# First FFN's pairs 5 to 17 as seven block products, and modulation pieces moved between stages

## The reference, cut to what matters

```python
mod = cond @ w_ada[l] + b_ada[l]
sh1, sc1, gt1, sh2, sc2, gt2, sh3, sc3, gt3 = ...   # nine rows of 1024
u = modulate(rms_norm(h, g_ffn1[l]), sh1, sc1)
h = h + 0.5 * gt1 * swiglu(u, w_ffn1_in[l], w_ffn1_out[l])
u = modulate(rms_norm(h, g_mix[l]), sh2, sc2)
h = h + gt2 * hybrid_mixer(u, w_in[l], ...)         # attention and gated delta net
u = modulate(rms_norm(h, g_ffn2[l]), sh3, sc3)
h = h + 0.5 * gt3 * swiglu(u, w_ffn2_in[l], w_ffn2_out[l])

def swiglu(u, w_in, w_out):
    a, b = jnp.split(u @ w_in, 2, axis=-1)          # 1024 -> 2 x 2816
    return (jax.nn.silu(a) * b) @ w_out
```

## Time and profile before

| | |
|---|---|
| median of 3 runs | 1198.42 us (1197.99 to 1198.63) |
| the profiled execution's own time | 1196.75 us |
| its span, first to last instruction | 1195.0 us |
| TensorE busy | 1179.7 us of 1195.0 |
| granted TensorE clock | 0.999 over the span |
| DVE, ACT busy | 826.4 us, 556.9 us |

### The profile page before, as it was taken

The page is one execution under the profiler, slowest core; times in us unless marked ns, Lnnn a source line. Parts: engine busy times, 40 slices in busy tenths (PEclk is TensorE's granted clock), DMA queues, the critical chain, the costliest instruction groups (busy, mean ns, idle before and its releaser), DMA issues.

```text
span 1195.0 us, 20070 instructions
## 1 busy us (share of the span) xinstructions
PE 1179.7 (99%) x7503; PEld 993.5 (83%) x7503; DVE 826.4 (69%) x1219; ACT 556.9 (47%) x843; POOL 60.3 (5%) x98
## 2 busy tenths in 40 slices
PE   7999999999999999999999999999999999999998
PEld 5788888888888887777787878888889999998887
DVE  5666676665665694777587566666789999988552
ACT  5423232322222585676773536544446666653331
POOL 1000000000111000000402110003000000000000
PEclk9999999999999999999999999999999999999999
DMA  9777666776564233221233132653233333342440
GB/s 326 230 205 210 199 176 187 210 211 192 160 167 115 56 104 89 71 54 53 71 89 91 53 96 66 211 153 95 71 106 106 106 105 103 102 132 78 115 115 27
DMA packets 235053, 152.51 MB, mean 128 GB/s; under 512 B 8021, under 2 KB 216046, under 8 KB 234990
## 3 DMA queue, kind: packets, MB, share of 16 engines
q1 hardware_dynamic: 230890, 149.62, 43.4%
q10 hardware_dynamic: 4100, 2.02, 0.6%
HBM read 145.31 MB, written 6.29 MB: 127 GB/s over the span
## 4 chain that ended last, share of the span: by engine, by line
PE 93%; DVE 3%; ACT 2%; DMA 1%; issue 1%; SPq 0%; ACTq 0%; DVEq 0%
PE tail L2224 8%; PE tail L2228 7%; PE tail L2233 7%; PE region L2224 7%; PE region L2233 7%; PE region L2228 7%; PE tail L2214 5%; PE region L2315 5%; PE region L2319 5%; PE region L2312 5%; PE tail L2216 5%; PE tail L2215 5%; PE region L2214 2%; PE region L2216 2%; PE region L2215 2%; PE tail L2312 1%
## 5 line engine op out<-in xcount | busy, mean ns | idle before, releaser
L785 ACT ACTIVATE w_hi<-raw 128x1024 fp32r<-128x1024 f32 (+1 forms) x160 | 179.1, 1119 | 359.7 <-PE region L2233 161.3
L1366 DVE TENSOR_TENSOR w_lo<-raw,w_hi 128x1024 fp32r<-128x1024 f32 (+1 forms) x158 | 205.9, 1303 | 92.5 <-ACT w_hi L785 92.4
L2214 PE MATMUL tail<-u_hi,w_hi 128*128 128x512 f32 x264 | 107.6, 408 | 0.9 <-DVE w_lo L1366 0.9
L2216 PE MATMUL tail<-u_hi,w_lo 128*128 128x512 f32 x264 | 103.2, 391 | 0.0
L2215 PE MATMUL tail<-u_lo,w_hi 128*128 128x512 f32 x264 | 103.0, 390 | 0.0
L2224 PE MATMUL region<-u_hi,w_hi 128*128 128x512 f32 x368 | 91.1, 390 | 0.1
L2233 PE MATMUL region<-u_hi,w_lo 128*128 128x512 f32 x368 | 90.9, 389 | 0.0
L2228 PE MATMUL region<-u_lo,w_hi 128*128 128x512 f32 x368 | 90.9, 389 | 0.0
L2224 PEld LDWEIGHTS region<-u_hi,w_hi 128*128 128x128 f32 x368 | 68.9, 188 | 15.2 <-issue 0.6
L2228 PEld LDWEIGHTS region<-u_lo,w_hi 128*128 128x128 f32 x368 | 69.1, 188 | 14.4
L2233 PEld LDWEIGHTS region<-u_hi,w_lo 128*128 128x128 f32 x368 | 69.1, 188 | 14.3
(11 more groups left out here) (492 smaller groups left out, 2332.7 us busy)
## 6 DMA issues: line engine op xcount, KB each, us to landing
raw<-in_w_ffn_in SPq DMA_DIRECT2D x168, 256.0 KB, 3.5
ada_raw<-in_w_ada SPq DMA_DIRECT2D x56, 512.0 KB, 5.2
raw<-in_w_in SPq DMA_DIRECT2D x90, 256.0 KB, 3.3
raw<-in_w_ffn_out SPq DMA_DIRECT2D x32, 384.0 KB, 5.3
raw<-in_w_ffn_out SPq DMA_DIRECT2D x32, 320.0 KB, 4.5
ada_early<-in_w_ada SPq DMA_DIRECT2D x8, 1024.0 KB, 10.7
gates<-kept_gates SPq DMA_DIRECT2D x16, 256.0 KB, 2.9
raw<-in_w_out SPq DMA_DIRECT2D x16, 256.0 KB, 3.2
```

Source lines behind the costliest of these rows:

```text
L785: act.activation(w_hi[:, slot % 2, 0:k, :], raw[:, slot, 0:k, :], ACT.Copy).then_inc(hi_ready, 1)
L1366: dve.tensor_tensor(w_lo[:, slot % 2, 0:k, :], raw[:, slot, 0:k, :], w_hi[:, slot % 2, 0:k, :].bitcast(f32), ALU.subtract).then_inc(lo_rea ...
L2214: pe.matmul(bank(b), wh, xh, start=start and n == 0, stop=False)
L2216: ins = pe.matmul(bank(b), wl, xh, start=False, stop=stop and n == k - 1)
```

## The change

Pairs 5 to 17 of the first FFN are mixed as those of the second. Their token sums are made at its start: `full` is written by ACT with the same activation that makes `u_hi` (8 activations in the chunk loop), the four sums, their splits and the copies stand in pairs 1 to 3. The modulation pieces leave pairs 1, 5 to 16; they stand one, two and one in pairs 2, 3, 4, then 2, 3, 4, 4, 3 in pairs 17 to 21, four in each of seven outputs, two around the merge and six in W_OUT. `ada_raw` has four buffers, its totals are added in four batches, and the rounds change their order. The loops of the first FFN keep only pairs 6 to 15 rolled.

```diff
-MOD_ROUNDS = (0, FF // P // 2 - 1, (MODS * KD - LATE) // 4)
+ROUNDS = (MODS * KD - LATE) // 4
+ROUND_AT = (0, 1, 4, 5, 2, 3) + tuple(range(6, ROUNDS))
+MOD_ROUNDS = (0, 4, 6, ROUNDS - 2, ROUNDS)
+PIECES = {2: (0,), 3: (1, 2), 4: (3,), 17: (4, 5), 18: (6, 7, 8), 19: (9, 10, 11, 12), 20: (13, 14, 15, 16), 21: (17, 18, 19)}
+OUT_PIECE = 20
+LAST_PIECE = OUT_PIECE + 4 * (D // P - 1)
...
-MIX_0, MIX_LAST = 5, KF - 1
+FULL_STEPS = KD, KD // 2
+MIX_0, MIX_LAST = (5, 5), (17, KF - 1)
...
-    return f == 1 and (not is_static(i) or MIX_0 <= 2 * i + jj <= MIX_LAST)
+    return not is_static(i) or MIX_0[f] <= 2 * i + jj <= MIX_LAST[f]
...
-                ada_raw = sb("ada_raw", [P, 2, ROWS, 4 * P], stack=t)
+                ada_raw = sb("ada_raw", [P, 4, ROWS, 4 * P], stack=t)
...
+                    for q in PIECES.get(2 * i + u // 2, ())[2 * (u % 2):2 * (u % 2) + 2] if is_static(i) else ():
+                        if q == 0:
+                            sp.wait_ge(t_step, tokens_done(0, FULL_STEPS[0] + 4))
+                        if q == 6:
+                            sp.wait_ge(glu_ready, MIX_LAST[0] + 1)
+                        load_piece(q, piece_slot(q), q % 4)
...
-                        load_late(2 * KF + 4 * i + u - 2, u % 2, (u - 2) % 4)
+                        for k in range(2):
+                            slot = (2 * u + k) % 4
+                            load_piece(OUT_PIECE + 8 * i + 2 * u + k, slot, slot)
...
+                if n == W_OUT:
+                    sp.wait_ge(unit_done, W_OUT)
+                if n in (MERGE, MERGE + 1) or W_OUT <= n < W_OUT + 6:
+                    q = LAST_PIECE + (n - MERGE if n < W_OUT else 2 + n - W_OUT)
+                    load_piece(q, piece_slot(q), q % 4)
...
                     early_part(k + 2)
+                for k1 in (k, k + 1):
+                    act.activation(full[0][:, k1, :], work[:, k1 % 2, :], ACT.Identity,
+                                   bias=mod[:, SH[0] * KD + k1:SH[0] * KD + k1 + 1]).then_inc(t_step, 1)
+                if k + 2 < KD:
...
+            def tokens(f, j, place):
+
+                if not is_static(j):
+                    return
+                for n in ((0,), (1,), (2, 3))[place]:
+                    if j == 1 + f:
+                        token_sums(f, n)
+                    if f and j == 3:
+                        tokens_lo(f, n)
+                if f == 0 and j in (2, 3) and place:
+                    tokens_lo(f, 2 * (j - 2) + place - 1)
...
+            def in_pieces(j):
+
+                for q in PIECES.get(j, ()):
+                    if q and q % 4 == 0:
+                        ada_rows(q // 4 - 1)
+                    piece(q, piece_slot(q), q % 4)
+
+            def out_pieces(o, slots):
+
+                for slot in slots:
+                    piece(OUT_PIECE + 4 * o + slot, slot, slot)
+
+            def last_piece(n):
+
+                q = LAST_PIECE + n
+                piece(q, piece_slot(q), q % 4)
+                if q % 4 == 3:
+                    ada_rows(q // 4)
...
+            ada_rows(OUT_PIECE // 4 - 1)
...
+            last_piece(0)
...
+            last_piece(1)
...
+                    if o < 6:
+                        last_piece(2 + o)
...
+                if k:
+                    dve.wait_ge(t_step, k - 1)
...
+            ada_totals(3)
```

More of the change, by code:

```diff
@@ L91, in mod_batch @@
 def mod_batch(row):
-    return 1 if (row * KD + KD - LATE) // 4 <= MOD_ROUNDS[1] else 2
+    own = [ROUND_AT.index((row * KD - LATE) // 4 + n) for n in range(2)]
+    return next(n for n in range(1, 5) if max(own) < MOD_ROUNDS[n])
 def first_tile(k):
@@ L138, in mixes, with nth, pairs_mixed @@
 def mixes(f, i, jj):
-    return f == 1 and (not is_static(i) or MIX_0 <= 2 * i + jj <= MIX_LAST)
-def nth(i, jj, steps, name, before):
-    return 2 * len(steps) * i + (len(steps) * (jj - MIX_0) + before + steps.index(name) + 1)
-def counted(i, jj, name, first, steps, last):
+    return not is_static(i) or MIX_0[f] <= 2 * i + jj <= MIX_LAST[f]
+def nth(f, i, jj, steps, name, before):
+    return 2 * len(steps) * i + (len(steps) * (jj - MIX_0[f]) + before + steps.index(name) + 1)
+def pairs_mixed(f):
+    return MIX_LAST[f] - MIX_0[f]
@@ L150, in counted @@
+def counted(f, i, jj, name, first, steps, last, former):
     j = 2 * i + jj if is_static(i) else None
-    if j == MIX_0 and name in first:
-        return first.index(name) + 1
+    before = len(first) + former
+    if j == MIX_0[f] and name in first:
+        return former + first.index(name) + 1
     if name + "+" in steps:
-        return nth(i, jj - 1, steps, name + "+", len(first))
-    return nth(i, jj, steps, name, len(first)) if j != MIX_LAST else \
-        nth(i, jj, steps, steps[0], len(first)) + last.index(name)
@@ L159, in copied @@
[L159 to L171, removed]
+        return nth(f, i, jj - 1, steps, name + "+", before)
+    return nth(f, i, jj, steps, name, before) if j != MIX_LAST[f] else \
+        nth(f, i, jj, steps, steps[0], before) + last.index(name)
+def copied(f, i, jj, name):
+    return counted(f, i, jj, name, FIRST_COPIES, MIX_COPIES, LAST_COPIES,
+                   f * (len(FIRST_COPIES) + len(MIX_COPIES) * pairs_mixed(0) + len(LAST_COPIES)))
@@ L411, in sq_low, with piece_slot, pieces_in @@
             return att_hi.rearrange("p e n -> p (e n)")[:, (2 + n % 2) * S:(2 + n % 2) * S + S]
+        def piece_slot(q):
+            return q % 2 if q < 4 else 3 if LAST_PIECE <= q < LAST_PIECE + 2 else q % 4
+        def pieces_in(q, slot):
+            if not is_static(q):
+                return 16 * ((q - slot) // 4 + (2 if slot < 2 else 1))
+            return 16 * (sum(piece_slot(p) == slot for p in range(q + 1)) + (slot >= 2))
         def parts_of(s):
@@ L897, in mixed_pair @@
[L897 to L903 removed]
+                    act.activation(w_hi[:, mix_a[f], low_half, :], raw[:, next_a, low_half, :], ACT.Copy).then_inc(hi_ready, 1)
@@ L1683, in ffn_in @@
                                           ALU.subtract).then_inc(g_lo_ready, 1)
-                        if turn:
-                            for n in (2, 3):
-                                token_sums(n) if jj == 0 else tokens_lo(n)
-                        if f == 0:
-                            if not (is_static(j) and j == 0):
-                                for k in range(2):
-                                    ada_late(2 * j - 2 + k, k, 2 * (1 - jj) + k, j)
+                        tokens(f, j, 2)
+                        if f == 0 and is_static(j):
+                            in_pieces(j)
             def ffn_out(s, f, phase):
```

486 lines of the change are left out of this document (264 added, 222 removed).

## The result

| | before | after |
|---|---|---|
| median of the runs | 1198.53 us (1197.99 to 1200.25) | 1190.48 us (1190.36 to 1190.70) |
| the profiled execution's own time | 1196.75 us | 1190.7 us |
| its span | 1195.0 us | 1189.0 us |

The ratio is 0.9931 (95% interval 0.9913 to 0.9948): faster, 8.05 us by the medians, but 6.0 us by the two profiles. The median of before is that of four runs here; in the three later rounds of experiments, of 7 to 18 runs, it was 1198.46 to 1198.65, so medians of different rounds can be compared. The 8.05 and the 6.0 both need an explanation.

A forecast was written before the change was run, and what follows sets the result against it. TensorE's own list was taken as the bound, busy 1179.7 of 1195.0 us. Terms -10.8 + 0.8 + 1.3 + 1.7 + 0.4 + 0.1 = -6.5 us, from 1198.42 to 1191.9 us; range 1187.5 to 1196.0.

The forecast's parts named there:

- 13 mixed pairs: First FFN, pairs 5 to 17: each takes 10.06 instead of 10.89 us on TensorE, 10.8 us gained.
- start: First FFN's start: ACT's writes of `full` delay splits and product, so pair 2 starts 0.8 us later (0.3 to 1.2).
- into the mixing: Pairs 3 to 6, first FFN: late splits cost TensorE 1.3 us (0 to 3); from pair 6 0.7 a pair regained.
- pairs 17 to 21, output stage: First FFN's last pairs and the outputs: added pieces and loads fit in the slack, no cost (0 to 2 us).
- merge: Third merge unit: piece 48, loaded ahead of the gates, shifts them by 2.2 us; 1.7 us lost (0 to 4).
- W_OUT and totals: W_OUT: DVE about 0.4 us late at the last residual (0 to 1.5); two more batches of totals on TensorE, 0.1 us.
- The base: Starting time for the sum: median 1198.42 us, taken to stand 1.7 us over the profiled execution.
- Rivals: Here, loads or DVE fall behind in pairs 17 to 21 and outputs: 1198.2 us, about 1195.5 in the middle; chance 0.15.

The follow-up runs named there:

- full_later: Changed kernel with ACT's last two activations into `full` placed behind the first weight split of the FFN; 1191.91 us.
- gates_first: Changed kernel with the load of modulation piece 48 issued behind the first four gate loads instead of ahead of them; 1191.23 us.
- piece_in_mixed: Changed kernel with modulation pieces 4 and 5 and the round's end before them in mixed pair 16 instead of plain pair 17; 1195.67 us.
- all_three: Changed kernel with `full` behind the first weight split, gate loads ahead of piece 48, and pieces 2, 1, 0 in pairs 2-4, 2, 4 in 17-18; 1189.87 us.
- link_first: Changed kernel with `full` behind the first weight split and, in the mixer's first half, GpSimd's coupling product between its two masked products; 1192.11 us.
- best: Changed kernel with `full` behind the first split, GpSimd's coupling between masked products, pieces 2, 1, 0, 2, 4, piece 48 one unit before the merge; 1189.75 us.

## Why the prediction was right, and where it was not

1190.48 was measured, 1191.9 predicted, within the range. By its steps, against the first profile of before:

| step | predicted | measured |
|---|---|---|
| 13 mixed pairs | -10.8 | -10.9 (10.89 to 10.05), and 0.83 for each of six pairs taken back |
| start | +0.8 | +0.5 from the span's start, +0.7 from `tok` (0.4 by `full_later`) |
| into the mixing | +1.3 | +2.2 |
| pairs 17 to 21, output stage | 0 | +0.1 in the seven plain pairs, no wait in the outputs |
| mixer | none | +0.6, issue |
| merge | +1.7 | +1.0; +0.2 against the other two profiles |
| W_OUT and totals | +0.5 | +0.4, all of it the totals: 0.2 around the outputs, 0.2 in W_OUT |
| sum | -6.5 | -6.0 (the rounded rows give 6.1) |

The sum is nearer than its terms: the way into the mixing and the mixer cost 1.5 us more than forecast, the start, the merge and W_OUT with the totals 1.1 less. That these cancel is luck.

- **The pairs** held because the pace was read from the second FFN's same form and not from columns. By the rule for isolated matmuls of the page "TensorE: Matmul & The Clock Gate" of the Trainium skill, section "Back-to-back issue gap", the pair would have been 9.17 us, an estimate; 10.05 was measured.
- **Into the mixing** is the term that was mis-sized, by 0.9 us. For pair 5 it was right: 1.24 us lost where 1.3 were forecast, most of it at the third product (ACT's split and then DVE's), 0.26 at the last one (forecast 0.3). The step that failed is the sentence that from pair 6 on 0.7 us a pair are regained, which leaves no loss in pair 6: it lost 0.96. DVE wasn't idle once from 78.78 to 107. Its splits for the third products of pairs 5 and 6 start 10.91 us apart (87.66 and 98.57), which is the 9.35 of a mixed pair and the 1.53 of piece 3, and TensorE needs only 10.05 for a pair. So a piece costs its own time less one pair's slack, on top of what the pair before had lost, and the forecast had counted that only at pair 5's last product. A backlog has to be followed through every product that comes before the slack has been earned.
- **Merge**: the shift was right, its price depends on what else is late. Before, DVE waits for a stored gate anyway in two of the three profiles, which hides most of it.
- **The mixer** was missing. Its places of idle time without a semaphore lie at other instructions after the change: 0.4 us before, 0.23 and 0.89 after. The longer one is 0.88 or 0.89 at the same instruction in three profiles (after, `gates_first`, `piece_in_mixed`) and 0.33 or 0.34 in seven others, so in part it goes with the version of the code; but the three profiles of the kernel before have 0.4, 1.6 and 0.9 in all with the same code. What causes it stays open.
- **The base** was wrong: I carried the profile's distance from the median, 1.7 us, over to the new kernel. It belonged to three stalls that this one profile had missed. After's median lies 0.2 us below its profiled execution, so the base was 1.9 too high; the sum was 0.5 too favourable, and 1.4 us are left by which the forecast was high.
- **Rivals**: TensorE waited for neither loads nor DVE in pairs 17 to 21 and the outputs. DVE wasn't idle once from 240.22 to the end of pair 21, but its splits still came in time.

## What to carry over

Where a tuned kernel is bound by one engine, count what each moved operation does to the backlog of the engine next in line, and follow that backlog through every product until it is earned back. Read small changes by stage and not by the total, and profile the kernel before more than once: a single profile can lack stalls that its median has. When a wait is removed by reordering a queue, look at which operation is behind it in the consumer's own list.

## What the hardware showed

- After TensorE had stood for 1.1 to 3.6 us its clock was 0.50 (1.2 GHz) for 3.4 us in three profiles (`before`'s second, `full_later`, `piece_in_mixed`), about 1.6 us more on top of the stall. The same wait of 1.1 us in `all_three`, `link_first` and `best` was followed by no drop: a stall's price can double, but not always.
- A shift of 0.3 us decides whether DVE or GpSimd is stretched where they overlap (0.65 to 1.55 us, 3.58 to 4.12 us), and only one of the two was on TensorE's path.
